# The first opening over pairs of tiles, 0.5 MB less fetched ahead of the weights, and one low part moved from GpSimd to VectorE

## The reference

```python
def _swiglu(h, w_up, w_down):
    gate, up = jnp.split(h @ w_up, 2, axis=-1)
    return (jax.nn.silu(gate) * up) @ w_down

def _layer(x, l, P, past_k, past_v, s_gla0, s_ret0):
    h = _rms_norm(x, P['ffn1_norm_pre'][l])
    x = x + 0.5 * _rms_norm(_swiglu(h, P['ffn1_w_up'][l], P['ffn1_w_down'][l]), P['ffn1_norm_post'][l])
    h = _rms_norm(x, P['mix_norm_pre'][l])
    m, k_rows, v_rows, s_gla, s_ret = _mixer(h, l, P, past_k, past_v, s_gla0, s_ret0)
    x = x + _rms_norm(m, P['mix_norm_post'][l])
    h = _rms_norm(x, P['ffn2_norm_pre'][l])
    x = x + 0.5 * _rms_norm(_swiglu(h, P['ffn2_w_up'][l], P['ffn2_w_down'][l]), P['ffn2_norm_post'][l])
```

## Time and profile before

| | us |
|---|---|
| median of 3 runs | 1365.83 (1365.51 to 1367.72) |
| the profiled execution, own time | 1364.96 |
| its span, first to last instruction | 1363.2 |
| PE busy | 1331.2 (98%) |
| DVE busy | 819.3 (60%) |
| ACT busy | 637.1 (47%) |
| POOL busy | 130.7 (10%) |

### The profile page before, as it was taken

How to read it: one execution, slowest core, us unless ns; L and a number is a source line. 1 busy time by engine, 2 the same in 40 slices (tenths; PEclk the granted TensorE clock), 3 DMA queues, 4 the chain that set the end, 5 groups by cost and what they waited for, 6 DMA issues and landing times.

```text
span 1363.2 us, 24696 instructions
## 1 busy us (share of the span) xinstructions
PE 1331.2 (98%) x9613; PEld 1292.3 (95%) x9613; DVE 819.3 (60%) x1230; ACT 637.1 (47%) x1001; POOL 130.7 (10%) x131
## 2 busy tenths in 40 slices
PE   5999999999999999999999999999999999999998
PEld 5999999988889999999999999999888899999998
DVE  5755544687666855554485555448866678555542
ACT  5544433653456644434464443346435565444433
POOL 2000000361000300000030000004600020000000
PEclk9999999999999999999999999999999999999999
DMA  7555555543344455544544554455333345544552
GB/s 185 171 164 171 164 164 148 155 120 86 91 119 122 124 146 147 154 143 142 162 123 144 150 153 140 146 161 148 91 86 91 101 124 155 154 146 147 146 151 66
DMA packets 351753, 187.49 MB, mean 138 GB/s; under 512 B 6320, under 2 KB 348604, under 8 KB 351688
## 3 DMA queue, kind: packets, MB, share of 16 engines
q1 hardware_dynamic: 348368, 177.49, 45.8%
q0 software_dynamic: 2480, 8.10, 1.7%
q10 hardware_dynamic: 840, 0.99, 0.3%
HBM read 182.24 MB, written 4.33 MB: 137 GB/s over the span
## 4 chain that ended last, share of the span: by engine, by line
PE 92%; DVE 4%; DMA 1%; ACT 1%; issue 1%; DVEq 1%; ACTq 0%; POOL 0%; SPq 0%; POOLq 0%
PE ps L634 28%; PE ps L636 28%; PE ps L635 28%; DVE w_l L513 1%; DMA raw<-in_ffn_w_up_dram 1%; PE ps L930 1%; PE ps L829 1%; PE ps L804 1%; PE ps L943 1%; DMA par_in<-in_ret_norm_dram 0%; PE ps L902 0%; DVE probs L1478 0%; PE ps L687 0%; DVE z L1537 0%; DVE y L1320 0%
## 5 line engine op out<-in xcount | busy, mean ns | idle before, releaser
L634 PE MATMUL ps<-xn_l,w_h 128*128 128x320 f32 x1840 | 579.4, 315 | 4.0 <-DVE xn_l L1309 3.6
L636 PE MATMUL ps<-xn_h,w_h 128*128 128x320 f32 x1840 | 567.9, 309 | 0.0
L635 PE MATMUL ps<-xn_h,w_l 128*128 128x320 f32 x1840 | 567.8, 309 | 0.0
L513 DVE TENSOR_TENSOR w_l<-raw,w_h 128x1024 fp32r<-128x1024 f32 (+1 forms) x340 | 410.7, 1211 | 168.3 <-ACT w_h L504 168.1
L504 ACT ACTIVATE w_h<-raw 128x1024 fp32r<-128x1024 f32 (+1 forms) x342 | 353.4, 1035 | 235.2 <-DMA raw<-in_ffn_w_down_dram 129.1
L634 PEld LDWEIGHTS ps<-xn_l,w_h 128*128 128x128 f32 x1840 | 345.1, 188 | 14.6 <-DVE xn_l L1309 5.4
L635 PEld LDWEIGHTS ps<-xn_h,w_l 128*128 128x128 f32 x1840 | 345.3, 188 | 1.5
L636 PEld LDWEIGHTS ps<-xn_h,w_h 128*128 128x128 f32 x1840 | 345.1, 188 | 0.0
L634 PE MATMUL ps<-hid_l,w_h 128*128 128x320 f32 x704 | 217.3, 309 | 0.0
L635 PE MATMUL ps<-hid_h,w_l 128*128 128x320 f32 x704 | 217.3, 309 | 0.0
L636 PE MATMUL ps<-hid_h,w_h 128*128 128x320 f32 x704 | 217.3, 309 | 0.0
(11 more groups left out here) (242 smaller groups left out, 1118.3 us busy)
## 6 DMA issues: line engine op xcount, KB each, us to landing
raw<-in_ffn_w_up_dram SPq DMA_DIRECT2D x176, 512.0 KB, 3.8
raw<-in_ffn_w_down_dram SPq DMA_DIRECT2D x64, 448.0 KB, 3.8
raw<-in_w_in_dram SPq DMA_DIRECT2D x54, 512.0 KB, 3.8
raw<-in_ffn_w_down_dram SPq DMA_DIRECT2D x32, 512.0 KB, 4.0
raw<-in_w_out_dram SPq DMA_DIRECT2D x16, 512.0 KB, 4.0
const<-in_tables_dram POOLq DMA_DIRECT2D x8, 298.0 KB, 4.6
x_in<-in_x_prompt_dram SPq DMA_DIRECT2D x1, 1024.0 KB, 6.3
scores<-in_cache_diff_k_dram POOLq DMA_DIRECT2D x2, 512.0 KB, 5.4
```

The source lines that it names most:

```text
L513: dve.tensor_tensor(w_l[s][:, 0:cols], raw[s][:, 0:cols], w_h[s][:, 0:cols], ALU.subtract).then_inc(w_lo, 1)
L634: pe.matmul(out, w_h[s][:, w], xl, start=first, stop=False)
L635: pe.matmul(out, w_l[s][:, w], xh, start=False, stop=False)
L636: return pe.matmul(out, w_h[s][:, w], xh, start=False, stop=last)
```

## The change

The third block of `x_in` no longer gets the last 64 prompt rows, and PE turns only its lower half, 64 rows into 64 columns; `x_loaded` is awaited at 3 x 16 for that. `diff_lambda` is fetched by ACT behind `xn_h` 7. POOL makes low part 0 only; DVE makes low part 1 behind `xn_l` 0, 2 behind `xn_l` 3 and 3 behind `xn_l` 5; ACT makes high part 2 behind `xn_h` 3 and high part 3 behind `xn_h` 5. The opening of the first sub-layer goes over tiles 0 and 1 for all eight k, and then over tiles 2 and 3, with the statistic's matmul before the last two k of the second pair. The five other sub-layers keep their opening.

```diff
-            sp.dma_start(x_in[0:64, 2, :], ins["x_prompt"][0, TOK[2]:T_P, :]).then_inc(x_loaded, 16)
             sp.dma_start(x_in[64:128, 2, :], ins["x_sample"][0]).then_inc(x_loaded, 16)
...
-            for v in range(2):
-                lo(pool, 0, v)
+            lo(pool, 0, 0)
...
+            def first_opening(u0):
+
+                for pair in range(0, OPENING, 2):
+                    for i in range(KD):
+                        if pair and i == KD - 2:
+                            stat_x(0, 0)
+                        if not pair:
+                            pe.wait_ge(xn_lo, i + 1)
+                        for t in (pair, pair + 1):
+                            if i == 0:
+                                pe.wait_ge(w_lo, u0 + t + 1)
+                            tile_part(slot(0, u0 + t), t, i, i + 1)
...
-                opening(l, u0, n, m)
+                if l * 3 + m:
+                    opening(l, u0, n, m)
+                else:
+                    first_opening(u0)
...
-            pe.wait_ge(x_loaded, 4 * 16)
+            pe.wait_ge(x_loaded, 3 * 16)
...
-                for i in range(3):
-                    mm = pe.transpose(ps[:, X_IN_BANK[k % 3], TOK[i]:TOK[i] + P], x_in[:, i, k * P:(k + 1) * P], C("ident"))
-                mm.then_inc(x_mm, 1)
+                for i in range(2):
+                    pe.transpose(ps[:, X_IN_BANK[k % 3], TOK[i]:TOK[i] + P], x_in[:, i, k * P:(k + 1) * P], C("ident"))
+                pe.transpose(ps[:, X_IN_BANK[k % 3], T_P:T], x_in[64:P, 2, k * P:(k + 1) * P], C("ident")[64:P, 64:P]).then_inc(x_mm, 1)
...
-                    if l == 0 and n == 0 and k < 2:
-                        hi(act, l, u0 + k + 2)
+                    if l == 0 and n == 0 and k in (3, 5):
+                        hi(act, l, u0 + (2 if k == 3 else 3))
+                    if l == 0 and n == 0 and k == KD - 1:
+                        fetch_lambda()
...
                     if l == 0 and n == 0 and k == 0:
-                        dve.wait_ge(w_lo, 2)
-                        lo(dve, l, 2)
-                        lo(dve, l, 3)
+                        dve.wait_ge(w_lo, 1)
+                        lo(dve, l, 1)
+                    if l == 0 and n == 0 and k in (3, 5):
+                        lo(dve, l, 2 if k == 3 else 3)
```

More of the change, by code:

```diff
@@ L1010, in _, with fetch_lambda @@
             act.dma_start(a2[:, :, :], ins["w_gla_a2"].rearrange("l r c -> r l c")).then_inc(lam_loaded, 16)
-            act.dma_start(lam_in[:, :, :, :].rearrange("p l a b -> p (l a b)"),
-                          ins["diff_lambda"].rearrange("(o l) a b -> o (l a b)", o=1).broadcast_to([P, DEPTH * 4 * DK_D])
-                          ).then_inc(lam_loaded, 16)
+            def fetch_lambda():
+                act.dma_start(lam_in[:, :, :, :].rearrange("p l a b -> p (l a b)"),
+                              ins["diff_lambda"].rearrange("(o l) a b -> o (l a b)", o=1).broadcast_to([P, DEPTH * 4 * DK_D])
+                              ).then_inc(lam_loaded, 16)
             def tile(t, k):
```

## The result

| | us |
|---|---|
| before, median of 20 | 1365.55 (1364.54 to 1367.72) |
| changed, median of 20 | 1369.17 (1367.67 to 1372.67) |
| ratio | 1.0026, 95% interval 1.0019 to 1.0032 |

The forecast was 1364.9 us, with a range of 1363.3 to 1366.6; the measured time lies above it, on the side that I gave 0.05. One of the executions of the kernel before that were made beside the experiments took 5129 us, against 1363 to 1370 for the others; it is left out everywhere. The page of the changed kernel answers to the earlier trace rows: 3.1 us more of span, with the same shares in the chain to a percent.

The account below looks back on a forecast made before the run. TensorE bounds the kernel (92% of the chain), so only its gap-free start can move. Between gains of 0.15 (same landing) and 1.4 us (rows 0.3 earlier) it took 0.9: 1365.83 - 0.9 = 1364.9 us, range 1363.3 to 1366.6.

Parts of the forecast that it names:

- Narrower turning: Turning x on TensorE: two of six turnings go from 128 to 64 columns, saving 0.2 us, or 0.
- The pace of the products: Opening products on TensorE at 0.1465 us each; 81 behind tile 1's start take 11.87 + 0.13 = 12.0 us.
- the marker: Start of the statistic's matmul, 31.37 before; 29.6 by the pair sum without stalls, 30.0 to 31.2 as the sign.
- Low part 1 to VectorE: GpSimd, with one low part, is done before 15.2; the first xn_l takes 0.55 us, not 1.77.
- The pair opening: TensorE needs only units 0 and 1 first; tile 1 starts at 17.6 instead of tile 3's 20.24, gaining 1.8 us.
- The meeting: GpSimd's additions from 20.8 hold VectorE's low part 3 and xn_l 6 and 7, 0.3 to 0.8 us each.
- the same-landing case: Parameter rows land as before; three VectorE instructions meet additions, giving back 1.65 of 1.8 us, gain 0.15.
- my sum for ScalarE: High parts, xn_h and squares from 13.35 us: a step to 19.8, the sixth square ending near 20.75.
- 0.5 MB less: Two 256 KB transfers leave: first high parts 0.9 to 1.8 us sooner, last parameter row taken 0.3 earlier.
- Lambda, and all behind the opening: Lambda's later fetch arrives at 28.2, free; after the opening costed at nothing, no new wait from 32 to 60 us.
- The rivals: No meeting, 0.15; parameter rows 1.9 us sooner, 0.08; rows later, 0.12 and 0.04; pair opening not acting, 0.03.
- rival 3: Parameter rows fall behind one or two more weight units: 1366.6 us (chance 0.12) or 1368.4 (0.04).

Follow-up runs that it names:

- The narrow turning alone: Kernel before with only the third turning cut to 64 rows into 64 columns, all transfers kept: 1367.41 us, ratio 1.0013, marker 33.50.
- the full turning: Changed kernel with the third block's upper half zeroed by VectorE and all three turnings 128 x 128: 1367.51 us, ratio 1.0010, marker 32.35.
- the gap filled: Changed kernel with four unread 256-column float32 matmuls before TensorE's wait for the parameter rows: 1369.91 us, ratio 1.0026, marker 34.75.
- the second of before: Kernel before, unchanged, profiled a second time: 1365.23 us (1 run), marker 31.45.
- no meeting, filled: Full-turning kernel with GpSimd's three first-opening additions on VectorE, plus 5, 3 and 2 unread TensorE matmuls: 1364.24 us, ratio 0.9980, marker 29.16.
- the order alone: Changed kernel with x_in, its turnings and lambda's fetch as before, leaving only the new order: 1367.03 us, ratio 1.0006, marker 32.08.
- the filled kernels: Kernels with unread TensorE work around the turnings; with identity turnings, the full-turning kernel took 1368.21 us (1.0012), the kernel before 1367.90 (1.0010).
- the two forms of full-row turning: Changed kernel with zeroed upper half: three 128 x 128 turnings, 1367.51 us; or sample rows by matmul of 128 rows against 64 identity columns, 1368.68.
- x sooner: Kernel before with the 256 KB of repeated prompt rows replaced by zeros, turnings full: 1365.87 us, ratio 0.9999, marker 30.07.

## Why the prediction was wrong, step by step

- **Narrower turning (the step that failed).** "0.2 us, if time goes by columns (0 if it doesn't)" had the wrong sign and no bound on that side. A 64-row turning between two 128-row ones costs 0.27 us per k, and the six k behind the parameter rows took 5.5 us where the full rows took 3.50: 1.6 of the 2.0 us are the shape (6 x 0.27), the rest the level of the last turnings. The narrow turning alone shows the 0.91 again, the full turning 0.64, the gap filled 0.57 against 0.43. The first `xn_l` came 2.7 us after my 15.94. Whether the shape also keeps TensorE at the low level is not shown: in the three profiles with it and no filling TensorE rose at 23 to 25 us, and in six of the seven with full rows and no filling before the first product, but in the seventh (the second of before) only at 20.5. The Trainium skill has the rule that speaks against the change and that I had not weighed: "TensorEngine Tiling (Array Packing)", section "Key Properties", says that a change of tiling mode (not merely of tile) drains TensorE. The 0.27 us more per k, with one 64-row tile between full ones in each, is in line with that; the page gives no price, and no run separates a drain from a slow load of the weights.
- **The pace of the products (the second step that failed).** I took 0.1465 us for each of them from the rows of before and never asked what it hung on. From 20.36 to 23.95 there are 13 products in 3.59 us, which at full pace, with 0.13 to restart, are 2.03: 1.56 us lost. With the two short stops (25.28 and 27.34, 0.57 us with their restarts) that makes the 34.48 - 20.36 = 14.1 us against my 12.0. The 2.8 us of the later start and these 2.1 are the 4.9 between my 29.6, which had no stops, and 34.48. This step fails without the narrow turning too: the full turning loses 1.5 us by it, and its median is 1.0 us above before where I had forecast 0.9 below. Where all products ran at 0.147 and no addition met them (no meeting, filled), the marker stood 12.2 us behind tile 1's start, as against my 12.0.
- **Low part 1 to VectorE.** The rows came as said: `xn_l` 0 took 0.55, and GpSimd was done at 13.4. But that it won anything is not shown: in the second profile of before GpSimd made both low parts, was done at 16.89, and `xn_l` 0, issued at 17.05, took 0.55 as well. The hold of 1.77 us depended on how TensorE's pace and the landing of the weights fell together.
- **The pair opening.** Right in mechanism: TensorE waits for `xn_l` 0 and low part 1. In the full-turning kernel tile 1 starts at 18.23 for my 17.6, and in the filled one without a meeting at 16.97. A gain from it in the median was not shown by the order alone (0.9998 to 1.0015).
- **The meeting.** Right: low part 2 or 3 and `xn_l` run long beside GpSimd's additions, and taking them away gave 0.54 us at the marker. The size, 1.65 us for the same-landing case, was three times the 0.54 measured, and twice the 0.8 at full pace: the additions met `xn_l` 4 and 5 and low part 3, and neither of the last two `xn_l` (24.62: 1.00 us for both). In the changed kernel the products were so slow that only the 0.57 us of stops were left. In my sum for ScalarE the step to 19.8 holds three squares and not the two named; its end, the sixth square at 20.75, came at 20.63.
- **0.5 MB less.** Right in the main: unit 1's high part began at 12.04 (my 12.3), and the last parameter row landed at 12.22, with no movement (I took 0.3 earlier). Over all profiles TensorE turned the parameters at 11.6 to 12.3 us with 256 or 512 KB less (the gap filled aside), and at 12.0 to 12.3 with all of it, so a movement of 0.3 is not excluded.
- **Lambda, and all behind the opening.** Right: no new wait.
- **The rivals.** None of the four was this one. The only one that ended on the slower side (rival 3) had the parameter rows landing later, and they didn't move.

What stays open: by what the 64-row turning costs its 0.27 us, what makes TensorE fall to the low level among the first products, where the filled kernels lose their time in the executions that weren't profiled, and the 1.2 us between the two forms of full-row turning.

## What to carry to other kernels

Before a partial-array matmul or turning is put among full ones, its cost is bounded on both sides: here the tile of fewer rows was the dearer one, and the full tile with zeros the faster. Where TensorE starts late or with gaps, take the spacing of its matmuls at that place, not from the steady part, and don't trust the granted clock's column before its first entry. A gain of a microsecond at the start is the size of one stretch at the low level, so compare medians of many runs, or runs of like mean clock, before believing one trace.

## What the runs showed of the hardware that I had not expected

- A turning of 64 rows between those of 128: 0.91 us for the three at the low level, against 0.64 with three full ones; 0.57 against 0.43 at the upper.
- TensorE at the low level with the granted clock's column at 1.00, before its first rise: 16 products in a stretch of 4 us instead of 25.
- TensorE fell to the low level among the first products after stops of 1.3 and 0.43 us in the full-turning kernel (18.48 to 21.92); in x sooner, after stops of 1.29 and 0.43, it did not.
- Fetching 512 KB less at the start (256 KB ahead of the weights, 256 KB in ScalarE's queue) moved ScalarE's first high part from 11.64 to 9.94 us, and the 2 KB parameter row not at all (12.21 and 12.22).
